# Last norm's scaled chunks made in the last phase, norm parameters on another queue, one weight split earlier: a two-layer encoder kernel on one core

## The reference

```python
def rmsnorm(x, g):
    y = x * rsqrt(mean(x * x, axis=-1, keepdims=True) + EPS)
    return y * g

for l in range(2):
    h = rmsnorm(x, g_mix[l])
    proj = h @ w_in[l]                      # split into q, k, v of three head groups and a gate cf
    o_a = diff_attention(...)               # 4 heads, normed by a_subln
    o_b = sliding_window_sink_attention(...)
    log_f = log_sigmoid(cf + c_fbias[l])    # gate of the third group, cumulated over the tokens
    o_c = forgetting_attention(..., log_f)
    x = x + concat([o_a, o_b, o_c]) @ w_out[l]
    h = rmsnorm(x, g_mlp[l])
    x = x + square(relu(h @ w_up[l])) @ w_down[l]
return rmsnorm(x, g_final)
```

## Time and profile before

| what | us |
|---|---|
| median of three runs (2528.42 to 2536.18) | 2529.07 |
| the profiled execution | 2525.3 |
| its span, first to last instruction | 2523.5 |
| PE busy | 2388.8 (95% of the span) |
| DVE busy | 1707.2 (68%) |
| ACT busy | 1119.9 (44%) |
| POOL busy | 269.5 (11%) |
| share of PE in the chain that ended last | 78% |

### The profile page before, as it was taken

The page is one execution under the profiler, slowest core; times in us unless marked ns, Lnnn a source line. Parts: engine busy times, 40 slices in busy tenths (PEclk is TensorE's granted clock), DMA queues, the critical chain, the costliest instruction groups (busy, mean ns, idle before and its releaser), DMA issues.

```text
span 2523.5 us, 32747 instructions
## 1 busy us (share of the span) xinstructions
PE 2388.8 (95%) x11857; PEld 1936.7 (77%) x11857; DVE 1707.2 (68%) x3130; ACT 1119.9 (44%) x1984; POOL 269.5 (11%) x287
## 2 busy tenths in 40 slices
PE   7999899899899989999999989998999999799997
PEld 6877777678788877888878777776777888688886
DVE  5555666666877768888636556666577777697873
ACT  5554444553444433333436544454454444333333
POOL 1111011123000000000221111121220000000003
PEclk9999999999999999999999999999999999899999
DMA  5201011211344467868331000102114444787753
GB/s 171 76 26 26 18 26 34 67 51 48 117 145 144 152 216 247 270 191 263 126 88 30 26 26 18 34 26 67 59 42 159 142 154 157 239 274 237 222 178 98
DMA packets 289928, 296.06 MB, mean 117 GB/s; under 512 B 19510, under 2 KB 236640, under 8 KB 289512
## 3 DMA queue, kind: packets, MB, share of 16 engines
q1 hardware_dynamic: 284056, 278.24, 35.0%
q10 hardware_dynamic: 5712, 15.73, 1.6%
HBM read 212.10 MB, written 81.82 MB: 116 GB/s over the span
## 4 chain that ended last, share of the span: by engine, by line
PE 78%; DVE 8%; issue 4%; ACT 4%; DMA 2%; DVEq 2%; POOL 0%; SPq 0%; ACTq 0%; POOLq 0%
PE ps L1883 23%; PE ps L2150 19%; PE ps L2202 8%; PE ps L2203 8%; PE ps L2204 8%; PE ps L2016 3%; PE ps L1963 3%; PE ps L2046 2%; PE ps L2036 1%; DVE probs L1393 1%; ACT probs L1018 1%; DVE probs L1421 1%; ACT pt_both L1036 1%; PE ps L2048 1%; DMA b_saved<-v_tile 1%
## 5 line engine op out<-in xcount | busy, mean ns | idle before, releaser
L2202 PE MATMUL ps<-b_hi,d_hi 128*128 128x512 f32 x896 | 350.7, 391 | 10.7 <-DVE d_lo L1685 10.6
L1883 PE MATMUL ps<-wide_hi,w_hi 128*128 128x512 f32 x1024 | 339.5, 413 | 21.2 <-POOL w_lo L871 6.3
L2204 PE MATMUL ps<-b_hi,d_lo 128*128 128x512 f32 x896 | 349.9, 391 | 0.0
L2203 PE MATMUL ps<-b_lo,d_hi 128*128 128x512 f32 x896 | 349.9, 391 | 0.0
L1883 PE MATMUL ps<-wide_lo,w_hi 128*128 128x512 f32 x1024 | 321.6, 396 | 0.0
L1883 PE MATMUL ps<-wide_hi,w_lo 128*128 128x512 f32 x1024 | 319.2, 393 | 0.0
L1444 DVE TENSOR_TENSOR pt_both<-ps,pt_both 128x512 fp32r<-128x512 f32 (+3 forms) x216 | 126.4, 585 | 222.8 <-ACT pt_both L1036 222.0
L1140 ACT ACTIVATE d_hi<-d_raw 128x1024 fp32r<-128x1024 f32 x112 | 118.4, 1058 | 338.3 <-DVE d_raw L1674 110.8
L1036 ACT ACTIVATE pt_both<-ps 128x512 fp32r<-128x512 f32 (+3 forms) x216 | 110.4, 511 | 337.6 <-PE ps L2016 337.3
L871 POOL TENSOR_TENSOR w_lo<-w_raw,w_hi 128x256 fp32r<-128x256 f32 x216 | 164.4, 792 | 830.2 <-ACT w_hi L921 830.2
L1018 ACT ACTIVATE probs<-probs,neg_max,slope 128x256 f32<-128x256 f32 (+7 forms) x256 | 202.3, 791 | 95.3 <-DVE neg_max L1408 75.2
(11 more groups left out here) (204 smaller groups left out, 4471.6 us busy)
## 6 DMA issues: line engine op xcount, KB each, us to landing
b_raw<-b_saved SPq DMA_DIRECT2D x112, 512.0 KB, 6.6
d_raw<-in_w_down_dram SPq DMA_DIRECT2D x112, 512.0 KB, 6.3
a_raw<-in_w_up_dram SPq DMA_DIRECT2D x60, 512.0 KB, 4.2
b_saved<-c_rows SPq DMA_DIRECT2D x120, 256.0 KB, 4.4
w_raw<-in_w_in_dram SPq DMA_DIRECT2D x92, 256.0 KB, 3.3
b_saved<-far SPq DMA_DIRECT2D x32, 512.0 KB, 4.2
w_raw<-in_w_out_dram SPq DMA_DIRECT2D x36, 256.0 KB, 3.0
x_saved<-xt ACTq DMA_DIRECT2D x16, 512.0 KB, 2.6
```

Source lines behind the costliest of these rows:

```text
L1883: mm = T.matmul(ps[p][:, bass.ts(t, BANK)], w, h[:, bass.ts(t, BANK)], start=(start and n == 0), stop=(stop and n == 2))
L2202: T.matmul(out, w0, b0, start=first, stop=False)
L2203: T.matmul(out, w0, b1, start=False, stop=False)
L2204: mm = T.matmul(out, w1, b0, start=False, stop=last)
```

## The change

- The seven parameter loads go from SP's queue to ACT's, ahead of its three quarters of x.
- `split_load(l, 3)` on ACT stands right behind `part_high(1)`, ahead of Exp and Ln instead of behind them.
- In the last layer `finish(k)` also writes the chunk times the gain into one of eight buffers `y_rows` (in the freed upper half of a region). The loop that wrote `turn_in` is gone.
- The last of the eight additions to `sq_sum` moves from POOL to DVE.
- PE turns chunks 0 and 1 as soon as the results of the last steps 0 and 1 are added, and turns into four PSUM banks instead of three.
- Of the rows, chunks 2, 5 and 7 are multiplied by ACT (eight instructions of 128 by 128 each), the other five by DVE as before. SP's stores wait for both.

```diff
-    FINAL_PS = (0, 1, 3)
+    FINAL_PS = (3, 0, 1, 2)
+    BY_ACT = (2, 5, 7)
-        turn_in = [place(f"turn_in{i}", [P, S], REGION_AT[0] + (48 + 4 * i) * KB) for i in range(2)]
+        y_rows = [place(f"y_rows{c}", [P, S], REGION_AT[0] + (32 + 4 * c) * KB) for c in range(NC)]
 # SP
-            sp.wait_ge(setup_pool, 1)
-            ... seven sp.dma_start into par_raw
-                sp.wait_ge(rows_done, 2 * (i + 1))
+                sp.wait_ge(rows_done, sum(1 for c in range(2 * i + 2) if c not in BY_ACT))
+                if any(c in BY_ACT for c in range(2 * i + 2)):
+                    sp.wait_ge(rows_scaled, sum(1 for c in range(2 * i + 2) if c in BY_ACT))
 # POOL
-                for k in range(NC):
+                for k in range(NC - (n == 2 * DEPTH - 1)):
 # ACT
+            act.wait_ge(setup_pool, 1)
+            ... seven act.dma_start into par_raw
                 part_high(1)
+                split_load(l, 3)
                 act.drain()
                 A.activation(g_tmp, g_tmp, ACT.Exp, scale=-1.0)
                 act.drain()
                 A.activation(g_tmp, g_tmp, ACT.Ln, bias=1.0).then_inc(gate_log, 1)
-                split_load(l, 3)
                     if l + 1 < DEPTH:
                         spill(c)
+                        return
+                    A.activation(y_rows[c][:], xt[:, c], ACT.Copy,
+                                 scale=param[:, 2 * DEPTH * NC + c:2 * DEPTH * NC + c + 1]).then_inc(y_ready, 1)
-            for c in range(NC):
-                if c == 4:
-                    root_mean_square(2 * DEPTH - 1)
-                if c >= 2:
-                    act.wait_ge(y_turned, c - 1)
-                A.activation(turn_in[c % 2][:], xt[:, c], ACT.Copy,
-                             scale=param[:, 2 * DEPTH * NC + c:2 * DEPTH * NC + c + 1]).then_inc(y_ready, 1)
+            root_mean_square(2 * DEPTH - 1)
+            act.wait_ge(rms_inverted, 2 * DEPTH + 1)
+            for c in BY_ACT:
+                act.wait_ge(y_turned, c + 1)
+                for b in range(NQ):
+                    e = A.activation(rows[:, b, c * P:(c + 1) * P], ps[FINAL_PS[c % 4]][:, b * P:(b + 1) * P], ACT.Copy,
+                                     scale=rms_col[:, b:b + 1])
+                e.then_inc(rows_scaled, 1)
 # DVE
+            dve.wait_ge(squared, NC * 2 * DEPTH)
+            dve.wait_ge(sq_added, NC * 2 * DEPTH - 1)
+            V.tensor_tensor(sq_sum[:], sq_sum[:], sq_one[:], ALU.add).then_inc(sq_added, 1)
             invert_rms(2 * DEPTH)
 # PE
-            pe.wait_ge(d_added, OUTS * DEPTH)
             for c in range(NC):
                 if c == 2:
                     sum_squares(2 * DEPTH - 1)
-                pe.wait_ge(y_ready, c + 1)
+                if c == 3:
+                    pe.wait_ge(rms_done, 2 * DEPTH + 1)
+                pe.wait_ge(y_ready, KORD.index(c) + 1)
+                pe.wait_ge(d_added, OUTS * DEPTH - 2 if c < 2 else OUTS * DEPTH)
```

More of the change, by code:

```diff
@@ L434, in hybrid_encoder @@
         rows_done = sem("rows_done")
+        rows_scaled = sem("rows_scaled")
         part_hi = sem("part_hi")
@@ L940, in rms_to_rows @@
                 A.activation(inv_rms[:], ps[2][:], ACT.Copy).then_inc(rms_out, 1)
+            act.wait_ge(setup_pool, 1)
+            r = 0
+            for l in range(DEPTH):
+                for g in (g_mix, g_mlp):
+                    act.dma_start(par_raw[r:r + NC, :], g[l].rearrange("(c p) -> c p", p=P)).then_inc(par_loaded, 16)
+                    r += NC
+            act.dma_start(par_raw[r:r + NC, :], g_final.rearrange("(c p) -> c p", p=P)).then_inc(par_loaded, 16)
+            act.dma_start(par_raw[NPAR:NPAR + DEPTH, :], a_subln).then_inc(par_loaded, 16)
+            act.dma_start(par_raw[NPAR + DEPTH:NPAR + 2 * DEPTH, F_ROW:P], c_fbias).then_inc(par_loaded, 16)
             for i in range(1, 4):
@@ L1853, in _ @@
             for c in range(NC):
+                if c in BY_ACT:
+                    continue
                 dve.wait_ge(y_turned, c + 1)
-                V.tensor_tensor(rows[:, :, c * P:(c + 1) * P], ps[FINAL_PS[c % 3]][:].rearrange("p (b d) -> p b d", d=P),
+                V.tensor_tensor(rows[:, :, c * P:(c + 1) * P], ps[FINAL_PS[c % 4]][:].rearrange("p (b d) -> p b d", d=P),
                                 rms_col[:].unsqueeze(2).to_broadcast([P, NQ, P]), ALU.mult).then_inc(rows_done, 1)
@@ L2221, in _ @@
                     sum_squares(2 * DEPTH - 1)
-                pe.wait_ge(y_ready, c + 1)
-                if c >= 3:
-                    pe.wait_ge(rows_done, c - 2)
-                turn(turn_in[c % 2], ps[FINAL_PS[c % 3]], NQ, y_turned)
+                if c == 3:
+                    pe.wait_ge(rms_done, 2 * DEPTH + 1)
+                pe.wait_ge(y_ready, KORD.index(c) + 1)
+                pe.wait_ge(d_added, OUTS * DEPTH - 2 if c < 2 else OUTS * DEPTH)
+                if c >= 4:
+                    before = c - 4
+                    if before in BY_ACT:
+                        pe.wait_ge(rows_scaled, BY_ACT.index(before) + 1)
+                    else:
+                        pe.wait_ge(rows_done, sum(1 for o in range(before + 1) if o not in BY_ACT))
+                turn(y_rows[c], ps[FINAL_PS[c % 4]], NQ, y_turned)
 _INS = ["x", "w_in", "a_lambda", "a_subln", "b_sinks", "c_fbias", "w_out", "g_mix", "g_mlp", "w_up", "w_down", "g_final"]
```

## The result

| | before | after |
|---|---|---|
| median, us (six runs each) | 2527.66 (2524.49 to 2536.18) | 2514.49 (2512.87 to 2515.44) |
| ratio, 95% interval | | 0.994 (0.9927 to 0.9953) |
| profiled execution, us | 2525.3 | 2515.44 |
| its span, us | 2523.5 | 2513.6 |

The change makes the kernel 13.2 us faster, 0.6%; 16.25 were forecast, and the time of 2514.49 lies 1.7 above the forecast of 2512.8. The two profiled executions differ by 9.9 only: the one of before lies 2.36 under the median of before, and the one of after, the longest of its six, 0.95 above its own.

What follows compares the result with a forecast made beforehand. PE, on the chain for 78%, was taken to bound the kernel: 3.4 (start) + 6.3 (stalls) + 4.75 (clock) + 1.8 (end) = 16.25 us off 2529.07 gives 2512.8, own range 2508 to 2516.

Steps and rivals of the forecast that it cites:

- The stalls, 6.3: Fourth slab, both layers: PE's wait of 3.13 us for POOL's `w_lo` goes, 6.3 us together.
- The clock behind them, 4.75: Fourth slab, both layers: without the idle time PE keeps full clock, 1.85 and 2.9 us, together 4.75.
- The start, 3.4: Kernel start: parameters on ACT's queue bring the chain up to ACT's first `wide_hi` forward, 3.4 us.
- The lower bound of 1.3: Kernel start: least gain, 1.3 us, if the first quarter of x still lands at 8.14.
- a first `wide_hi` after 12: Kernel start: sign that the start term is wrong, ACT's first `wide_hi` coming later than 12 us.
- The rival of the shared transfer: Kernel start: ACT's quarters still take half the DMA engines, start gains only 1.3 us, 2514.9 in all; chance 0.12.
- the time of SP's issues, 2.5: Kernel start: by the skill's rule on DMA queues only SP's seven issues are saved, some 2.5 us, 2513.7 in all.
- a gain by a higher clock: Kernel start: PE waits less and keeps the higher clock over its first products, 3 us more, 2509.8; chance 0.04.
- The end, 1.8: Kernel end: earlier last addition and turning of chunks 0 and 1 bring the first rows and stores forward 1.8 us.
- Dividing the rows: Kernel end: sharing the last rows between DVE and ACT costs and brings nothing, since the stores set the end.
- The slower rival: Last four steps: scaled copies on ACT delay the last units' weights, up to 24.1 us lost, 2537; chance 0.03.
- The stall that moves: Behind the fourth slab: PE waits there instead or its clock falls anyway, half of 11.05 us lost, 2518.3; chance 0.09.

Runs made afterwards that it cites:

- Kernel 12: Kernel before with one wait added: DVE starts its three gate steps only after POOL has split the fourth slab's weights; 2517.11 us against 2529.96, ratio 0.9955.
- Kernel 2: Kernel before with only the seven parameter loads moved to ACT's queue, ahead of the quarters of x; 2528.75 us against 2528.09, ratio 0.9999.
- kernel 8: Changed kernel with all eight chunks of the last rows on DVE and none on ACT; ratio 0.995 to the kernel before.
- kernel 6: Changed kernel with the second quarter of x on SP's queue right behind the first; ratio 0.9954 to the kernel before.

## Why the prediction was right, and where it was not

- **The stalls, 6.3: right in size, half right in cause.** 3.13 went in each layer. The prediction saw POOL's 5.55 and 2.80 side by side and used them only as bounds for the new place; it put the stall down to the two table loads. Kernel 12 shows that the collision alone accounts for 2.7 of the 3.13. Moving `w_hi` does both at once, it starts POOL's work 5 us earlier against the end of the third slab and takes it out from beside the DVE steps; either would have been enough.
- **The clock behind them, 4.75: right.** It was 1.75 and 2.84 in the profiled pair (12.72 and 13.81 less 10.97), and 2.1 a layer over six stalls, so 4.2 would be the better figure. The prediction's 10.87 for a slab was 0.1 short, as its window begins 0.17 after the slab's first matmul. Kernel 12 adds that a wait of 0.4 costs no clock.
- **The start, 3.4: wrong.** This is the term that was mis-sized. Kernel 2 gives nothing, within a loss of 2.3 and a gain of 2.5, and the table's means show no gain at the third slab. The lower bound of 1.3 isn't excluded by that: the profiled pair itself ends the third slab 1.1 earlier, which lies inside the spread of the traces. Three steps failed, one after the other. The parameters were to land at 5.5: PE turned them at 7.89, 1.7 us earlier than before and not 3.9; their small pieces passed while SP's queue moved 1.80 MB. ACT's quarters of x were to be only "issued 3 us later": they also stood behind the small loads, moved from 7.46 us on, held ACT to 10.08 and, through the copy's issue, the first `w_hi` to 13.84. So the gain was 1.7 at the first `wide_hi` (11.43 against 13.11) and 0.8 at the first product. And the sum stopped at the first `wide_hi`; the next late thing, the second slab's load, was not asked for. The sign that was to show this, a first `wide_hi` after 12, stood too early in the chain to do so.
- **The rivals at the start.** The rival of the shared transfer had the direction and not the cause: ACT's queue took 2.8% of the DMA engines in the first 8 us, not half. Nor was the time of SP's issues, 2.5, won. The measured 2514.49 lies nearer to these two (2514.9 and 2513.7) than to the forecast, but the times can't tell the three apart. Of a gain by a higher clock nothing is left at the third slab either.
- **The end, 1.8: right.** 1.7 between the profiles of before and after, and the range of traces is 1.0 to 1.7, since PE's summing is sometimes slower. (The prediction's steps add up to 2505.0, a gain of 1.9, where it wrote 2505.1 and 1.8; the summing began when it said, 3.09 after the last addition, and took 1.95 instead of 1.69.) Dividing the rows brings nothing, as said (kernel 8).
- **The slower rival** fell: the `d_lo` of the second of the last four steps ended at 2478.2, 13.21 us ahead of the last unit's addition as before, so without even the delay of 1.2, and PE did not wait. **The stall that moves** fell too: PE has no new wait behind the fourth slab in either layer.
- **The sum.** Without the start, 6.3 + 4.2 + 1.7 = 12.2 against a measured 13.2, with an interval of 11.9 to 18.5 by the ratio. The forecast was held by the two terms read from waits of PE; its surplus of 3 us was the start. That the time came within 1.7 of the forecast is half luck: 1.4 of the surplus were hidden by the earlier median of before, which lay that much above the later one.

## What to carry to other kernels

A wait of PE costs more than its length where the clock falls behind it; a stall read from the trace, with the windows behind it, is a price one can trust. When an instruction takes twice as long in one place as in another, ask what ran beside it before asking what it waited for: here one wait on another engine was worth as much as the reordering. A gain at the start has to be followed to the first step that everything meets in, since a later load can take it back, as in kernel 2.

## What the runs showed of the hardware

- Small loads at the head of a queue went ahead of the large ones behind them: in all nine traces with the parameters on ACT's queue its first 1 KB piece of x starts after the last 512-byte piece of the parameters (7.46 and 7.05 us in after). That queue moved 0.04 MB in the first 8 us, and 0.96 MB without them. Whether the small pieces were slow by themselves or beside SP's 1.80 MB was not tried apart.
- The issue of three 1 MB loads held ACT 6.30 us instead of 4.68, and the next issue on that queue took 1.28 to 2.36 us in six traces. It took 0.35 with the parameters on SP, and also with only two such loads ahead of it (kernel 6).
- A POOL subtraction of four pieces of 128 by 256 took 5.55 us beside two DVE steps that read two tiles in SBUF, and 2.80 to 2.92 with at most 0.24 us of such a step beside it; beside a DVE step that reads PSUM a piece took 0.72 us, as long as alone.
- The stretches at 1.2 GHz move from one execution to the next of the same program: mean granted clock of 0.80 and 0.95 over the same 35 us. Two profiles of one execution each can't price 3 us by their spans; matched matmul by matmul, they show where it lies.
